# Expert stream of a decoder step: within a step, the two V rows before the two U rows

## What is computed

```
ue  = take(peer_u, eidx)                       # 128 rows of 1024 a token
act = gelu(einsum('thkd,td->thk', ue, xk))     # a dot product with each row
ve  = take(peer_v, eidx)                       # 128 rows of 1024 a token
out = einsum('thk,thkd->td', g * act, ve)      # weighted sum of the V rows
```

## Time and profile before

| | us |
|---|---|
| median of 3 runs | 4228.14 |
| lowest, highest | 4212.68, 4239.83 |
| the profiled execution | 4189.63 |
| its span, first to last instruction | 4187.5 |
| POOL busy in it | 2586.3 |
| VectorE busy in it | 2794.4 |
| TensorE busy in it | 2939.1 |

### The profile page before, as it was taken

One profiled execution on the slowest core, in us unless ns is written; L12 is line 12 of the kernel. 1 busy time (PEld: TensorE's weight loads), 2 busy tenths in 40 slices (PEclk: granted clock), 3 DMA queues, 4 the chain that ended last, 5 costly groups with the idle time before them and its releaser, 6 DMA issues.

```text
span 4187.5 us, 32801 instructions
## 1 busy us (share of the span) xinstructions
PE 2939.1 (70%) x9896; PEld 1826.7 (44%) x9896; DVE 2794.4 (67%) x5582; ACT 700.3 (17%) x1637; POOL 2586.3 (62%) x2172
## 2 busy tenths in 40 slices
PE   8778698666688767766767769866778645555555
PEld 7667575343355435534545535534545311111111
DVE  0441767565646998777656986777657986767665
ACT  1321113111211011321111111322111001001000
POOL 0021146655676476677777666677767667777776
PEclk9789799678899878878888979978889766767667
DMA  3114388867879788997899999898899989999998
GB/s 146 41 61 162 139 327 322 300 226 266 316 278 367 309 311 342 341 337 279 320 346 409 395 335 420 336 337 296 323 357 399 349 301 374 417 371 403 368 342 336
DMA packets 342239, 1298.80 MB, mean 310 GB/s; under 512 B 39480, under 2 KB 48720, under 8 KB 321936
## 3 DMA queue, kind: packets, MB, share of 16 engines
q0 software_dynamic: 297216, 1082.26, 68.9%
q1 hardware_dynamic: 44848, 214.44, 13.3%
HBM read 1278.87 MB, written 19.76 MB: 310 GB/s over the span
## 4 chain that ended last, share of the span: by engine, by line
POOL 32%; PE 27%; DVE 18%; issue 11%; DMA 9%; DVEq 2%; ACT 1%; ACTq 0%; SPq 0%; POOLq 0%
POOL ringb L535 28%; PE bank L847 12%; DMA ringb<-in_v,eidx 6%; PE vsum L759 5%; DVE ringb L1307 4%; PE bank L886 3%; DVE acc L1348 3%; PE bank L1024 2%; POOL arena L567 2%; DVE scT L1687 1%; PE bank L968 1%; DMA out_ss<-arena 1%; DVE Pbb L1403 1%; DVE bTb L1410 1%; DVE Pbb L1407 1%
## 5 line engine op out<-in xcount | busy, mean ns | idle before, releaser
L759 PE MATMUL vsum<-ringb,diag 128*128 128x512 f32 x2048 | 1304.5, 777 | 826.6 <-DMA ringb<-in_v,eidx 720.5
L535 POOL DMA_INDIRECT ringb<-in_u,eidx x1024 | 1247.7, 1218 | 871.6 <-DVE dg L1307 461.4
L535 POOL DMA_INDIRECT ringb<-in_v,eidx x1024 | 1140.4, 1114 | 370.2 <-issue 302.9
L1307 DVE CUSTOM_DVE_ANT_0 ringb<-ringb,n2t 128x1024 f32<-128x1024 f32 x1032 | 1259.8, 1248 | 124.0 <-DMA ringb<-in_u,eidx 58.9
L759 PEld LDWEIGHTS vsum<-ringb,diag 128*128 128x128 f32 x2048 | 449.0, 237 | 1529.9 <-issue 1283.4
L1348 DVE SCALAR_TENSOR_TENSOR acc<-ringb,wgt,acc 128x1024 f32<-128x1024 f32 x512 | 660.6, 1290 | 304.0 <-DMA ringb<-in_v,eidx 297.8
L847 PE MATMUL bank<-wring,nTb 128*128 128x256 f32 x3024 | 684.2, 386 | 1.8 <-issue 1.1
L847 PEld LDWEIGHTS bank<-wring,nTb 128*128 128x128 f32 x3024 | 553.8, 184 | 158.3 <-issue 49.3
L1061 ACT ACTIVATE diag<-cst,wgt 128x128 f32<-128x128 f32 x512 | 190.9, 394 | 693.6 <-PE vsum L759 427.5
L886 PE MATMUL bank<-nTb,wring 128*128 128x256 f32 (+1 forms) x1152 | 267.8, 391 | 7.8 <-DMA wring<-in_w 5.1
L886 PEld LDWEIGHTS bank<-nTb,wring 128*128 128x128 f32 x1152 | 225.9, 197 | 63.6 <-issue 21.9
(11 more groups left out here) (232 smaller groups left out, 2311.6 us busy)
## 6 DMA issues: line engine op xcount, KB each, us to landing
wring<-in_w SPq DMA_DIRECT2D x152, 1024.0 KB, 7.8
ringb<-in_u,eidx POOLq DMA_INDIRECT x1024, 6.3
ringb<-in_v,eidx POOLq DMA_INDIRECT x1024, 6.4
n2t<-scratch_n SPq DMA_DIRECT2D x16, 512.0 KB, 7.8
oab<-in_xp SPq DMA_DIRECT2D x4, 1024.0 KB, 12.1
bTb<-in_keysT SPq DMA_DIRECT2D x4, 1024.0 KB, 8.9
vgb<-in_xp SPq DMA_DIRECT2D x4, 1024.0 KB, 5.1
scratch_h<-vgb SPq DMA_DIRECT2D x4, 1024.0 KB
```

The costliest lines, as they stand in the source:

```text
L535: pool.indirect_dma_start(out=ring[r], out_offset=None, in_=a["u"] if kind == "u" else a["v"], in_offset=bass.IndirectOffsetOnAxis(ap=at, ...
L759: last = mm(out[:, g * 512:(g + 1) * 512], lhs, ring[r][:, g * 512:(g + 1) * 512], start=(k == 0), stop=(k == end))
L1307: v.tensor_tensor_reduce(out=ring[r], in0=ring[r], in1=n2t[:, n % 2, :], scale=1.0, scalar=0.0, op0=ALU.mult, op1=ALU.add, accum_out=dg[:, ...
```

## The change

In `ring_places` the slots of a step are given to the V rows first, in `pool_quad` the gathers of a step are issued v0, v1, u0, u1, and in `dve_quad` the block that takes v1 stands ahead of u0 and u1. TensorE's, ScalarE's and SP's programs are untouched; the ring, LAG, the marks and the number of instructions are the same.

```diff
@@ ring_places
-        for kind, at in (("u", q), ("v", q - LAG)):
+        for kind, at in (("v", q - LAG), ("u", q)):
@@ pool_quad
-            rows = [("u", 2 * q + j) for j in range(2)] if q < QU else []
-            if 0 <= q - LAG < QU:
-                rows += [("v", 2 * (q - LAG) + j) for j in range(2)]
+            rows = [("v", 2 * (q - LAG) + j) for j in range(2)] if 0 <= q - LAG < QU else []
+            if q < QU:
+                rows += [("u", 2 * q + j) for j in range(2)]
@@ dve_quad, this block moved from the end of the step to its beginning
+            x = 2 * (q - LAG) + 1
+            if 0 <= q - LAG < QU and x not in on_pe:
+                i, k = ITEMS[x]
+                m = group_of(i, k)
+                if k == 1:
+                    dve.wait_ge(d_h[i % 2], 16 * (i // 2 + 1))
+                else:
+                    row_used(dve, ("v", x - 2))
+                dve.wait_ge(wgt_ready, m + 1)
+                r = row_here(dve, ("v", x))
+                STT(acc[:, i % 2, :], ring[r], wgt[:, m % 2, k % GROUP:k % GROUP + 1], acc[:, i % 2, :], ALU.mult, ALU.add)\
+                    .then_inc(slot_used[r], 1)
```

More of the change, by code:

```diff
@@ L1337, in dve_quad @@
                     STT(y, y, f, gfb[0:R, :], ALU.mult, ALU.mult).then_inc(y_out, 1)
[L1338 to L1349, removed]
         def route_tile(dve, c, t, R, gap):
```

## The result

The changed kernel takes 4253.8 us (median of 16, 4234.2 to 4264.3) against 4218.0 us (median of 16, 4204.2 to 4239.8): ratio 1.0072, interval 1.0052 to 1.0091. It is slower by 36 us. The forecast was a gain of 35 us. In the experiments single executions ran slower at a lower granted clock; the ratios leave them out and the medians do not, so a ratio can differ by up to 0.4% from the quotient of two medians.

A forecast was written before the change was run, and what follows sets the result against it. No engine was taken as full; TensorE, VectorE and POOL hold each other up in turn. Tail 0, v0 -45, VectorE's rows 0, later endings +10: -35 us on the 4228.1 us median, 4193 us, range 4118 to 4270.

The forecast's parts named there:

- v0 for TensorE: Interleaved part, 600 to 3360 us: v0 gathered 2.48 to 4.13 us earlier, gain of 45 us, between 0 and 91.
- what is late next: Interleaved part: VectorE's rows come as late as before, so no gain where VectorE was as late as TensorE.
- hundred or more: Sign of being right: TensorE's waits for V rows, 600 to 3360 us, fall from 392.8 us by a hundred or more.
- The phase of these decides ... the phase should come out the same.: Tail: gathers and VectorE's operations keep their phase because the cycle is the same; cost 0, 6 us either way.
- u0, u1 and v1 for VectorE: VectorE's step: stall moves from v1 to the U rows, same in all; taken as 0, 71 us one way.
- What ends one operation later: A group's last dot and the sum at L1331 come 1.28 us later: 10 us of loss, between 0 and 35.
- Rival C: Projections and gla: TensorE's slot heads POOL's step, 64 us slower, 4292 us; mark POOL's TensorE waits above 100 us; chance 0.16.
- The mark on the tail: Sign of being wrong: the tail, from the last routing on, changes by more than 10 us.
- the mark for rival B: Sign of being wrong: TensorE's waits fall and the interleaved part is no shorter.
- Rival B: Whole kernel: transfers are the bound, so row order is of no account; 4228 us to within 10; chance 0.17.
- Rival A: Interleaved part: TensorE's wait was the pacemaker, every pass gains 4.13 us; 91 us, 4137 us; chance 0.22.

The follow-up runs named there:

- one-input pair: Kernel before and changed kernel, VectorE's dot and weighted sum each replaced by a sum over the one row: 3967.7 us (0.9566) and 3991.2 us (0.9630).
- POOL's order alone: Kernel before with only slots and POOL's gathers V rows first, VectorE's order as before: 4089.6 us against 4140.0, ratio 0.9869.
- two halves: The change split against the kernel before: slots and POOL's gathers V first, ratio 0.9869; only VectorE taking v1 first, ratio 1.0613.
- one-input forms: Kernels before and changed, stream operations replaced by one-row sums; with diagonals made two steps ahead, 4130.5 us (0.9788) and 4140.2 us (0.9816).
- VectorE's alone: Kernel before with only VectorE's order changed, v1 ahead of u0 and u1, slots and gathers as before: 4399.9 us, ratio 1.0613.
- gelu shift: A group's gelu and weights made one step later; on the kernel before with one-row sums 4132.7 us (0.9785), on the changed kernel 4249.5 us (1.0063).

## Why the prediction was wrong

**What failed.** The forecast was a gain of 35 us, the result a loss of 36, some 71 us apart. Two steps failed. The larger is "v0 for TensorE", a gain of 45 us, with its overlap ("what is late next"): what the earlier row gave, TensorE's other waits took back. The other is the held gathers, costed at nothing in the interleaved part. The one-input pair tells them apart: with no gather held behind the stream's operations, where only the prediction's own terms are at work, the new order still lost 23.5 us.

**v0 for TensorE, a gain of 45 us.** The first half of this step was right: TensorE's waits for V rows fell, by 59 us in the pair of profiles, and their landing lost two fifths of its share of the chain. Three things were wrong. The fall was smaller than the "hundred or more" asked for. The pass shown in the earlier trace rows was priced as if v0 could be gathered 4.13 us earlier because it no longer waits for VectorE; POOL then waits for TensorE in its stead (45 to 290 us). And "what is late next" was sought in VectorE's rows alone. It was in TensorE's own other waits: diagonal 31 to 70 us, tile's sum 29 to 46, and POOL's gla product 143 to 181, 94 us more for the 59 less. The one-input pair shows the same exchange with no gather held, 67 us less for 65 more. Which of the three waits carries the loss stays open. (The chain goes from such a landing to TensorE in 21 of the 22 passes, not in each.)

**"The phase of these decides ... the phase should come out the same."** I saw the longer gathers in the earlier trace rows, drew the bounds for the tail only, and argued there that two sequences with the same cycle have the same phase. For the tail the result was right on the chip where it was tried: 1.0002 with the new order there alone. But the argument leaves out the interleaved part, where the cycle is cut by the mixer and where most of the held time is: 360 of 452 us before. There the new order put the acc operation where a gather comes due, and held time rose by 107 us. The prediction had no term for that. How much it is worth net: the whole loss is 36 us here and some 37 on the chip of the one-input runs, where without holding 23.5 us of it are left. That leaves 12 to 14 us, an estimate that the intervals do not tell from nothing. Yet the holding is the larger lever, up to 4.3% in all on that chip, and it is what makes POOL's order alone win there. That the forecast was within 2% of the result all the same, with two halves of -1.3% and +6.1% that it knew nothing of, was luck.

**u0, u1 and v1 for VectorE, 0.** The end of a step is the same with both halves changed, and VectorE's waits for rows went from 98 to 136 us, not a large miss. But they did not go from V rows to U rows as the prediction has it: those for v1 stayed (75.2 to 73.8), those for U rose (22.9 to 61.7). What this hid is that the two halves are of opposite sign and large: -1.3% and +6.1%.

**What ends one operation later, 10 us of loss.** Gelu as a cause failed its test; the diagonals, which are ScalarE's too, may carry some 14 to 17 us in the one-input forms. If so the size was near by luck, and the name was wrong.

**Rival C** had the right sign and its mark was met: POOL's waits for TensorE passed 100 us. Its mechanism is not the cause all the same. POOL's waits in all fell from 490 to 417 us, and two kernels with another slot than TensorE's at the head won nothing. A mark that a wrong mechanism meets as well is a weak one. The mark on the tail was met too, 21 us in the two traces for the 10 allowed, and the mark for rival B, TensorE's waits lower and the interleaved part no shorter, says best what happened. **Rival B** may be true of some chips in the tail (below); that it did not matter for the difference is not shown there. **Rival A** fell: an earlier V row did not become time.

## What to carry to other kernels

When a profile shows instructions of one engine longer than their shortest, find out what they wait for inside before costing an order at nothing: match their ends with the other engine's, count the held time by stage, and give it a term. And take a change of order apart into its halves: here, on one chip, the kernel that only moves POOL's gathers is 1.3% faster, the one that also moves VectorE's operation is 0.9% slower. Compare stage times only between profiles of one chip. A stall removed from an engine is worth only what is left when that engine's next wait is put in its place.

## What the runs showed of the hardware that I had not expected

A gather issued by POOL is not slowed by VectorE in proportion. If it begins in the course of an operation with two SBUF inputs, it is held until that operation's end, and then takes its 0.94 us (less some 0.12), whatever VectorE starts next. At the edges it slips through: of the gathers of the kernel before that began in the last 0.13 us of a dot none of 155 was held, and of those in its first 0.05 us only 18 of 61; the gather at 3708.96 in the earlier trace rows, 0.01 us behind a dot's start, took 0.94. So some hundredths of a microsecond in phase decide between 0.94 and 1.98 us. In the tail this locks the two engines into a pattern, and on the chip of the experiments the pattern goes with the pace: 750 us with no gather held, 762 with POOL's order alone, 791 with the kernel before's order, 802 with the changed one, 921 with VectorE's alone, for the same rows.

Chips differ in how fast they carry the same gathers. On the chips where the kernel before took 4218 to 4222 us, the one-input form's tail took 828 us with nothing held, at this rate (POOL's gathers only):

```profile
3309.00:4137.00 828.00, 533.93 (x568) 0.72 0.94 364
```

364 GB/s, where the one-input form without the gelu shift reached 402 on the other chip. POOL stood there 26 times, 85 us, behind something that the profile only names "remote". The tail of the kernel before took 826 us with 92 us held, beside runs of 4218 us, so where it is so slow the holding seems to cost nothing in the tail, and what the one-input form gains (2.1%) it gains in the interleaved part (2709 us for 2761). It looks as if the transfers bound that tail; with a DMA share of 0.94, where the faster chip had 0.99, that is not shown. A kernel that is won by faster gathers wins less there: the form with 13 slots and POOL's order, with the shifted gelu, was at 0.9923, and the one without the shift at 0.9765 on another chip. Whether the shift has a part in this was not tried.
